# FFN gate and up by Strassen's scheme from column block 2 on, with its sums on VectorE and the down projection one gate block later

## The reference, cut to what matters

```python
def swiglu(h, w_gate, w_up, w_down):
    return (jax.nn.silu(h @ w_gate) * (h @ w_up)) @ w_down

x = x + swiglu(rms_norm(x, norm_ffn[l]), w_gate[l], w_up[l], w_down[l])
```

## Time and profile before

| what | value |
|---|---|
| time of 3 runs, median (lowest to highest) | 1870.86 us (1867.57 to 1871.2) |
| span of the profiled execution, slowest core | 1862.8 us |
| spans of the 8 cores | 1858.9 to 1862.8 us |
| TensorE matmul busy | 1723.7 us (93%), 10862 instructions |
| VectorE busy | 753.8 us (40%), 1521 instructions |
| ScalarE busy | 533.5 us (29%) |
| mean granted TensorE clock | 0.975 to 0.977 |

### The profile page before, as it was taken

How to read it: one execution, slowest core, us unless ns; L and a number is a source line. 1 busy time by engine, 2 the same in 40 slices (tenths; PEclk the granted TensorE clock), 3 DMA queues, 4 the chain that set the end, 5 groups by cost and what they waited for, 6 DMA issues and landing times.

```text
span 1862.8 us, 30031 instructions; the slowest of 8 cores (1858.9 to 1862.8 us)
## 1 busy us (share of the span) xinstructions
PE 1723.7 (93%) x10862; PEld 936.7 (50%) x10862; DVE 753.8 (40%) x1521; ACT 533.5 (29%) x921; POOL 102.2 (5%) x150
## 2 busy tenths in 40 slices
PE   4899999999986678997799999999999999999998
PEld 2565546666653237874344444444444444444444
DVE  3542124566566443434544151514325151423415
ACT  2442344877777352224450000000000000000000
POOL 0100000000001320000000000000000000000000
PEclk9899999999998889998899999999999999999999
DMA  9911634322316449147225507355270816446154
GB/s 219 250 47 24 115 69 78 77 53 41 81 42 135 127 113 210 46 81 122 46 46 91 91 12 125 49 88 86 50 123 14 136 28 109 63 74 104 32 91 181
DMA packets 40399, 166.17 MB, mean 89 GB/s; under 512 B 6208, under 2 KB 22208, under 8 KB 22336
## 3 DMA queue, kind: packets, MB, share of 16 engines
q0 software_dynamic: 17616, 111.32, 35.3%
q1 hardware_dynamic: 22640, 52.93, 9.2%
HBM read 258.18 MB, written 8.52 MB: 143 GB/s over the span
## 4 chain that ended last, share of the span: by engine, by line
PE 82%; DMA 5%; DVE 5%; ACT 4%; issue 3%; SPq 0%; POOL 0%; DVEq 0%; ACTq 0%; POOLq 0%
PE bank L1408 16%; PE pair L1405 16%; PE pair L1488 8%; PE bank L1488 8%; PE bank L521 5%; PE pair L521 4%; PE bank L1246 4%; DMA arena<-sel 3%; PE pair L850 3%; PE bank L829 2%; PE bank L698 2%; PE bank L703 2%; PE pair L1299 1%; PE pair L1246 1%; DMA arena<-wblk 1%
## 5 line engine op out<-in xcount | busy, mean ns | idle before, releaser
L1408 PE MATMUL bank<-arena 128*128 128x512 bf16 x1408 | 318.7, 379 | 0.0
L1405 PE MATMUL pair<-arena 128*128 128x512 bf16 x1344 | 303.8, 379 | 0.0
L1411 ACT ACTIVATE arena<-pair 128x512 bf16<-128x512 f32 x84 | 50.1, 597 | 806.4 <-PE pair L1405 786.6
L1412 DVE TENSOR_TENSOR arena<-bank,arena 128x512 bf16<-128x512 f32 x88 | 60.9, 692 | 537.9 <-PE pair L1405 411.0
L839 ACT ACTIVATE arena<-bank,arena 128x512 bf16<-128x512 f32 (+3 forms) x402 | 214.5, 573 | 72.0 <-PE pair L850 29.9
L1408 PEld LDWEIGHTS bank<-arena 128*128 128x128 bf16 x1408 | 137.6, 98 | 165.5
L1405 PEld LDWEIGHTS pair<-arena 128*128 128x128 bf16 x1344 | 131.5, 98 | 158.5
L1488 PE MATMUL pair<-arena 128*128 128x512 bf16 x704 | 166.3, 379 | 0.0
L1488 PE MATMUL bank<-arena 128*128 128x512 bf16 x704 | 166.3, 379 | 0.0
L850 PE MATMUL pair<-arena 128*128 128x129 bf16 (+1 forms) x1184 | 122.5, 223 | 17.2 <-DVE arena L843 15.0
L1491 DVE TENSOR_TENSOR arena<-pair,arena 128x512 f32<-128x512 f32 x176 | 121.8, 692 | 29.7 <-DVE arena L1491 23.8
(11 more groups left out here) (175 smaller groups left out, 1616.6 us busy)
## 6 DMA issues: line engine op xcount, KB each, us to landing
arena<-wblk POOLq DMA_DIRECT2D x106, 1024.0 KB, 12.5
arena<-xc SPq DMA_DIRECT2D x24, 1024.0 KB, 13.0
arena<-arena SPq DMA_DIRECT2D x64, 135.0 KB, 2.5
y<-arena SPq DMA_DIRECT2D x8, 1024.0 KB, 3.8
arena<-sel SPq DMA_DIRECT2D x28, 256.0 KB, 3.8
arena<-memb SPq DMA_DIRECT2D x2, 1024.0 KB, 5.5
arena<-cbf SPq DMA_DIRECT2D x1, 360.2 KB, 26.5
arena<-pvec SPq DMA_DIRECT2D x1, 219.0 KB, 9.9
```

Of the source, the lines that this page charges most:

```text
L1405: op(PE, lambda: nc.tensor.matmul(bank[pg][:, :], lhsT=wgt[:, kc, cc * 128:(cc + 1) * 128], rhs=hb[:, kc, :], start=(kc == 0), stop=(kc == ...
L1408: op(PE, lambda: nc.tensor.matmul(bank[pu][:, :], lhsT=wut[:, kc, cc * 128:(cc + 1) * 128], rhs=hb[:, kc, :], start=(kc == 0), stop=(kc == ...
L1412: op(DVE, lambda: nc.vector.tensor_tensor(out=actT[aj][cc][:, tc * 512:(tc + 1) * 512], in0=bank[pu][:, :], in1=sgt[sj][:, :], op=ALU.mult ...
```

## The change

From `jb` 2 on, each weight block (gate or up, 2048 x 256) times all 1024 activations is done as a 2 x 2 by 2 x 2 block product in Strassen's manner (Winograd's form): 7 products of half size, each 8 matmuls of 128x512 with a depth of 1024, so 56 matmuls where there were 64. The sums of activations are made once (`act_sums`, 3 VectorE instructions on 128x4096, and `act_diffs`, 2 of them in place). The sums of weights are made for every block by VectorE, 5 instructions of 128x1024 bf16 (`weight_sums`: three into `w3`, two in place in the slot), each emitted between the steps of the block before (`nxt`). The products go through four banks, here S, P, Q and R (banks 4 to 7); S, P and Q take two products each. Their combination takes one ScalarE copy and 6 VectorE instructions in fp32, then 4 times Silu (ScalarE, gate) or a multiply (VectorE, up). Gate and up of a `jb` now stand apart, one whole block of 56 matmuls after the other. The down projection of `jb` 2 and 3 runs after the gate block of `jb` 4, and so on; it is itself unchanged. The core of the diff:

```diff
+        def act_sums():
+            for k, (a, b) in enumerate((((0, 0), (1, 1)), ((0, 0), (0, 1)), ((1, 0), (1, 1)))):
+                op(DVE, lambda: tt_(out=b3[k], in0=B[a[0]][a[1]], in1=B[b[0]][b[1]], op=ALU.add), r=[h3[0][1], h3[1][1]], w=[b3b[k]] if k != 1 else [], pw=[b3b[k]] if k == 1 else [])
+        def weight_sums(n, wt, wb):
+            A = [[wt[:, 8 * k:8 * k + 8, 128 * f:128 * f + 128] for k in range(2)] for f in range(2)]
+            W, Wb = w3[n % 2], w3b[n % 2]
+            def s(k, a, b):
+                return lambda: op(DVE, lambda: tt_(out=W[:, k, :, :], in0=a, in1=b, op=ALU.add), r=[wb], w=[Wb[k]])
+            def d(a, b):
+                return lambda: op(DVE, lambda: tt_(out=a, in0=a, in1=b, op=ALU.subtract), r=[wb], pw=[wb])
+            return [s(2, A[0][0], A[0][1]), s(1, A[1][0], A[1][1]), s(0, A[0][0], A[1][1]), d(A[1][0], A[0][0]), d(A[0][1], A[1][1])]
+            product(S_, A[1][1], wb, B[1][0], Bb[1][0], True)
+            op(ACT, lambda: nc.scalar.copy(out=s4[:, :], in_=bank[S_][:, :]), r=[bankb[S_]], w=[s4b])
+            product(P_, W[:, 2, :, :], Wb[2], B[1][1], Bb[1][1], True)
+            op(DVE, lambda: tt_(out=dd[:, :], in0=s4[:, :], in1=bank[P_][:, :], op=ALU.subtract), r=[s4b, bankb[P_]], w=[ddb])
+            nxt()
+            product(S_, W[:, 1, :, :], Wb[1], B[0][0], Bb[0][0], False)
+            emit(bank[S_][:, :], bankb[S_], 1, 0)
+            nxt()
+            product(Q_, W[:, 0, :, :], Wb[0], b3[0], b3b[0], True)
+            op(DVE, lambda: tt_(out=ee[:, :], in0=bank[Q_][:, :], in1=dd[:, :], op=ALU.add), r=[bankb[Q_], ddb], w=[eeb])
+            op(DVE, lambda: tt_(out=ee[:, :], in0=ee[:, :], in1=bank[S_][:, :], op=ALU.subtract), r=[bankb[S_]], w=[eeb])
+            nxt()
+            product(P_, A[0][0], wb, B[0][1], Bb[0][1], False)
+            emit(bank[P_][:, :], bankb[P_], 0, 1)
+            op(DVE, lambda: tt_(out=ee[:, :], in0=ee[:, :], in1=bank[P_][:, :], op=ALU.add), r=[bankb[P_]], w=[eeb])
+            nxt()
+            product(R_, A[1][0], wb, b3[1], b3b[1], True)
+            op(DVE, lambda: tt_(out=ee[:, :], in0=bank[R_][:, :], in1=ee[:, :], op=ALU.add), r=[bankb[R_]], w=[eeb])
+            emit(ee[:, :], eeb, 1, 1)
+            nxt()
+            product(Q_, A[0][1], wb, b3[2], b3b[2], False)
+            op(DVE, lambda: tt_(out=cc_[:, :], in0=bank[Q_][:, :], in1=dd[:, :], op=ALU.add), r=[bankb[Q_], ddb], w=[ccb])
+            emit(cc_[:, :], ccb, 0, 0)
+        for jb in range(2, 22):
+            for gate in (True, False):
+                wt, wb, i = cur
...
+                    if gate:
+                        nx = wtaken()
+                    else:
+                        d_ = wtaken()
+                        nx = wtaken()
+                    todo = weight_sums(n + 1, nx[0], nx[1])
+                seven(n, wt, wb, aj, gate, todo)
+                wdone(i)
...
+                    if len(pairs) == 2:
+                        down(pairs)
+                        pairs = []
+                cur = nx
+        down(pairs, last=True)
```

More of the change, by code:

```diff
@@ L209, in buf @@
         return b
-    ARENA_BYTES = 204 * 1024
+    ARENA_BYTES = 207 * 1024
     def arena_init(self):
@@ L1454, in build @@
         rot_proj = Rot([0, 1, 2, 3])
[L1455 to L1480, removed]
+        FS = self.scope()
@@ new lines, in build @@
+        b3 = [HB[1][:, 8 * k:8 * k + 8, :] for k in range(2)] + [self.tile(FS, "b3", [128, 8, 512], BF16)]
+        b3b = [HBb[1], HBb[1], self.buf("b3")]
+        w3 = [self.tile(FS, f"w3_{j}", [128, 3, 8, 128], BF16) for j in range(2)]
+        w3b = [[self.buf(f"w3_{j}_{k}") for k in range(3)] for j in range(2)]
+        sg4 = sqt + [self.tile(FS, f"sg4_{j}", [128, 512], BF16) for j in range(2)]
+        sg4b = sqtb + [self.buf(f"sg4_{j}") for j in range(2)]
+        s4, dd, ee, cc_ = [self.tile(FS, n, [128, 512], F32) for n in ("s4", "dd", "ee", "cc")]
@@ new lines, in build @@
+        s4b, ddb, eeb, ccb = [self.buf(n) for n in ("s4", "dd", "ee", "cc")]
+        B = [[h3[t][0][:, 8 * k:8 * k + 8, :] for t in range(2)] for k in range(2)]
+        Bb = [[self.buf(f"B{k}{t}") for t in range(2)] for k in range(2)]
+        tt_ = nc.vector.tensor_tensor
+        def act_sums():
+            for k, (a, b) in enumerate((((0, 0), (1, 1)), ((0, 0), (0, 1)), ((1, 0), (1, 1)))):
+                op(DVE, lambda: tt_(out=b3[k], in0=B[a[0]][a[1]], in1=B[b[0]][b[1]], op=ALU.add), r=[h3[0][1], h3[1][1]], w=[b3b[k]] if k != 1 else [], pw=[b3b[k]] if k == 1 else [])
@@ new lines, in act_diffs @@
+        def act_diffs():
+            for (k, t), (k2, t2) in (((1, 0), (0, 0)), ((0, 1), (1, 1))):
+                op(DVE, lambda: tt_(out=B[k][t], in0=B[k][t], in1=B[k2][t2], op=ALU.subtract), r=[h3[t2][1]], w=[Bb[k][t], h3[t][1]])
+            for k in range(2):
+                _add(Bb[k][k].w, list(h3[k][1].w.values())[0])
+        def weight_sums(n, wt, wb):
[6 more added lines that the diff above has]
+            return [s(2, A[0][0], A[0][1]), s(1, A[1][0], A[1][1]), s(0, A[0][0], A[1][1]), d(A[1][0], A[0][0]), d(A[0][1], A[1][1])]
@@ new lines, in product, with seven, emit, nxt @@
+        def product(bi, lhs, lhsb, rhs, rhsb, fresh):
+            for k in range(8):
+                op(PE, lambda: nc.tensor.matmul(bank[bi][:, :], lhsT=lhs[:, k, :], rhs=rhs[:, k, :], start=(fresh and k == 0), stop=(k == 7), skip_group_check=True), r=[lhsb, rhsb], w=[bankb[bi]])
+        def seven(n, wt, wb, aj, gate, behind):
+            A = [[wt[:, 8 * k:8 * k + 8, 128 * f:128 * f + 128] for k in range(2)] for f in range(2)]
+            W, Wb = w3[n % 2], w3b[n % 2]
+            S_, P_, Q_, R_ = 4, 5, 6, 7
+            def emit(src, srcb, f, t):
+                j = 2 * f + t
+                if gate:
+                    op(ACT, lambda: nc.scalar.activation(out=sg4[j][:, :], in_=src, func=AF.Silu), r=[srcb], w=[sg4b[j]])
+                else:
+                    op(DVE, lambda: tt_(out=actT[aj][f][:, t * 512:(t + 1) * 512], in0=src, in1=sg4[j][:, :], op=ALU.mult), r=[srcb, sg4b[j]], w=[actTb[aj][f][t]])
+            def nxt():
+                if behind:
+                    behind.pop(0)()
+            product(S_, A[1][1], wb, B[1][0], Bb[1][0], True)
[21 more added lines that the diff above has]
+            emit(cc_[:, :], ccb, 0, 0)
+            while behind:
+                nxt()
@@ L1481, in build, with down @@
+        def down(pairs, last=False):
             for tt in range(8):
@@ L1485, in build @@
                     n_ = 0
-                    for (a_, wd_, wdb_, _) in dheld:
+                    for (a_, wd_, wdb_, _) in pairs:
                         for cc in range(2):
@@ L1491, in build @@
                     op(DVE, lambda: nc.vector.tensor_tensor(out=dst, in0=bank[psi][:, :], in1=dst, op=ALU.add), r=[bankb[psi]], w=[xrb[h][tt % 4][2 * cb4], xrb[h][tt % 4][2 * cb4 + 1]])
-                if jb == 21:
+                if last:
                     ob_ = self.buf(f"out{tt}")
@@ L1495, in build, with wtaken @@
                     self.outtoks.append((ob_.dsem, ob_.dcnt))
-            for d_ in dheld:
+            for d_ in pairs:
                 wdone(d_[3])
-            dheld = []
+        def wtaken():
+            wt, wb = wget()
+            return wt, wb, self.wcur - 1
+        act_sums()
+        for jb in range(2):
+            ia, (wgt, wgb_), ib, (wut, wub) = wgu[jb]
+            for cc in range(2):
+                drain(glu(jb, wgt, wgb_, wut, wub, cc, 1, rot_g.next(), rot_u.next()))
+            wdone(ia)
+            wdone(ib)
+        act_diffs()
+        pairs = []
+        for a_ in range(2):
+            wdt, wdb, i = wtaken()
+            pairs.append((a_, wdt, wdb, i))
+        cur = wtaken()
+        for f_ in weight_sums(0, cur[0], cur[1]):
+            f_()
+        down(pairs)
+        pairs = []
+        n = 0
+        for jb in range(2, 22):
+            aj = jb % 2
+            for gate in (True, False):
+                wt, wb, i = cur
+                todo = []
+                if gate or jb < 21:
+                    if gate:
+                        nx = wtaken()
+                    else:
+                        d_ = wtaken()
[3 more added lines that the diff above has]
+                wdone(i)
+                n += 1
+                if not gate:
+                    if jb == 21:
+                        d_ = wtaken()
+                    pairs.append((aj, d_[0], d_[1], d_[2]))
+                else:
+                    if len(pairs) == 2:
+                        down(pairs)
+                        pairs = []
+                cur = nx
+        down(pairs, last=True)
         self.mark("out")
```

## The result

The changed kernel takes 1946.1 us where the kernel before takes 1871.0 in the same comparison: ratio 1.0399, 95% interval 1.0378 to 1.042, slower by 75 us. The forecast was 1962 us, a loss of 91; the measured time lies in the range of 1920 to 2020.

What follows compares the result with a forecast made beforehand. The prediction took TensorE's matmuls to bound the kernel. Its terms, -69.1 + 111.6 + 14.8 + 26.3 + 5.9 + 1.5 = +91.0 us, on 1870.9 gave 1962 us, range 1920 to 2020.

Steps and rivals of the forecast that it cites:

- 320 matmuls: Gate and up blocks: 8 matmuls fewer in each of 40 blocks, at 0.2159 us each, -69.1 us.
- nine holds: Up block after a down projection: VectorE's weight sum waits for gt5 and TensorE stops, 9 x 12.4 = +111.6 us.
- clock in the gate block: Gate block after each TensorE stop for gt5: half clock costs 2.9 us, 9 x 2.9 = +26.3 us.
- steady waits: Next block's first product waits for the last in-place weight sum: 1.2 us per up, 0.25 per gate block, +14.8 us.
- start: First down projection: its adds wait on VectorE behind act_diffs and five weight sums, +5.9 us.
- end: Last down projection: its third matmul waits for the last combination and multiply, +1.5 us.
- The rival in which the clock stays up: TensorE keeps full clock after the nine stops for gt5: 1936 us, chance 0.15.
- VectorE's steady work: Up block's sums, combinations and multiplies laid out step by step on VectorE: next block starts 1.2 us late.
- the rival of 1.22 us: Each weight sum on VectorE takes 1.22 us, not 0.69: 59 us more, 2021 us, chance 0.15.
- the faster rival: In the up block after a down projection, gt5 lands before its wait stops TensorE: 1835 us, chance 0.03.
- The 8.1 us between span and time: Whole kernel: median of the runs lies 8.1 us above the 1862.8 us span, so the forecast starts from 1870.9.

Runs made afterwards that it cites:

- the first fill: The changed kernel with 36 unused matmuls ahead of the seventh product of nine up blocks, those where TensorE waits for gt5's sums: 1943.6 and 1940.2 us.
- the down projection at once: The changed kernel with the down projection again right after the up block of the odd column block: 1851.6 us, ratio 0.9907 to the kernel before.
- the run with the gate block first: The changed kernel with only the weight transfers reordered, the next gate block ahead of the down block: 1834.1 us, ratio 0.9821 to the kernel before.

## Why the prediction was right, and where a size was off

It forecast a slower kernel by one mechanism, and the runs show that mechanism: gt5 lands 17.5 us after the down projection in the period above (16.6 forecast), VectorE stands 13.06 us before its sum, TensorE stops after six products for 9.66 us. Over the nine periods of core 5 VectorE stands 11.8 us on average (12 forecast) and TensorE 8.4 (8.9 forecast). Taking only the transfers' order away gives back 112 us; the place of the down projection alone costs the kernel before 54.

The terms of the sum, with what core 5 measured:

| term | forecast | measured |
|---|---|---|
| 320 matmuls | -69.1 | 320 fewer, at 1.73 us for 8 as before: -69.1 |
| nine holds | 9 x 12.4 = 111.6 | 75.7 waiting for bank Q, 15.2 before the gate block, 14.4 for the seventh product at half clock, 2.9 of modelled ends: 108.2 |
| clock in the gate block | 9 x 2.9 = 26.3 | 1.56 to 1.97 in six of nine, nothing in three: 10.4 |
| steady waits | 14.8 | 10 x 1.02 + 11 x 0.21, 3.4 of modelled ends: 15.9 |
| start | 5.9 | 6.0, and 1.9 of half clock after it: 8.1 |
| end | 1.5 | 1.5 |

"Modelled ends" are 0.16 us for each pause: a pause is listed from the modelled end of a matmul, 0.16 us after the next one could have started. The measured column sums to 75.0 us, and the stage took 75.4 more. So the forecast of 91 was 16 us too high, and the clock is all of it: the holds came out 3 us shorter, the start and the steady waits 3 us longer.

- **The step that was mis-sized** is the clock: "I take that 2.9 us once a hold", 26.3 us in all, where 10.4 were measured. The clock did fall to 0.50 (1.2 GHz) in the hold, as in the earlier trace rows, but in the period above the gate block's first 24 matmuls took 6.90 us where 5.34 is full pace, 1.6 us more; and in three of the nine periods they took no more than full pace behind a like hold:

```profile
1158.45 5.34 PE L1491 MATMUL pair<-arena 128*128 128x512 bf16 x24 [1.61 <-DVE arena L1486]
```

  The windows view of core 5 over the end of the hold and the gate block's first 4.7 us (busy times, clock, DMA share, GB/s) shows the clock coming back within them:

```profile
1248.20:1251.00 2.80, 1.75 (x5) 0.68 (x6) 2.20 (x4) 0.00 (x0) 0.51 (x1) 0.50 1.08 164
1251.00:1254.00 3.00, 3.00 (x12) 1.20 (x11) 0.00 (x0) 0.59 (x1) 0.00 (x0) 0.76 1.03 167
```

  In the earlier trace rows 2.9 us were lost, which at 0.2159 us a matmul means half clock for some 13 of the 16; here it was 7 of 24. The rival in which the clock stays up was wrong too. Over all eight cores the gate block lost time behind 58 of 72 holds. The forecast also left out that the seventh product itself would run at half clock: it took 3.57 us out of the pause before the gate block, which was 1.6 to 2.0 us and not the 3.5 forecast, and so cost nothing.
- **The hold's length depends on the core.** The forecast took its landing from one period of one core. On cores 0, 2, 4 and 6 TensorE waited 53 to 55 us for bank Q in all, on 1, 3, 5 and 7 75 to 77. The slowest core sets the time. The one period read was of a core (7) that gets gt5 late, 15.8 us after its issue in that period; core 6 got it after 13.4 to 14.3. That the late kind was read is luck: the prediction did not look at the other cores.
- **VectorE's steady work**, laid out step by step from spacings of 0.60 and 0.79 us, was right within 0.2 us a block: the next block started 1.18 us late by count (1.02 of idle and 0.16 of modelled end), 1.2 forecast. The weight sums took 0.68 us, 0.69 forecast, by carrying the 256 to 512 element rows on to 1024; the rival of 1.22 us is out.
- **In place of the faster rival** stands its own condition, fulfilled by other means: once gt5 is issued early the kernel takes 1834 us, and the prediction had 1835 for a covered hold.
- **The 8.1 us between span and time** are not what lies around an execution. In the runs on record the time is 1.0 to 1.4 us above the span of the slowest core; so the profiled execution of the kernel before, with a span of 1862.8, was a short one of about 1864 us. The forecast isn't harmed by this, since it added its 91 us to the median of the runs.

## What to carry to other kernels

When work on the operands of the next step is put into an in-order engine's list in the middle of this step, the time by which that operand must have landed moves forward by a whole step, and everything behind the wait stops with it. So before such a change, list for each transfer when it can be issued (whose slot it takes, and what stands ahead of it in its queue) and when its first reader now comes; here two entries in the wrong order were worth 112 us, more than the 69 that the algorithm saves. And a dependency kept for a whole buffer is worth splitting where the reader and the writers touch different parts: 25 us here.

## What the runs showed of the hardware that was not expected

- In each pair of neighbouring cores (0 and 1, 2 and 3, and so on) one gets its weight blocks later than the other. The second block of five landed about 13 us after its issue on cores 0, 2, 4 and 6 in most periods and 15 to 17 on 1, 3, 5 and 7; the spans are 1915.7 to 1919.2 and 1939.4 to 1943.7 us. Which of the two is late differs from run to run: with the first fill, cores 1, 2, 4 and 7 were the late ones. In the kernel before, where TensorE waits for none of these blocks, the difference is there too on some pairs (second block after 13.4 to 14.3 us on core 6, 15.8 to 16.6 on core 7), and the profiled cores lie within 4 us of each other.
- Behind a pause in dense work the next matmuls sometimes run at half clock and sometimes don't, at the same length of pause. With the down projection at once, TensorE pauses nine times for 1.99 us on each core; 28 of these 72 pauses are followed by 1.5 to 1.7 us of lost time, the other 44 by none. Two of core 0 (the matmuls right behind the pause, then the next eight):

```profile
1251.80 1.46 PE L1543 MATMUL bank<-arena 128*128 128x512 bf16 x6 [1.99 <-DVE arena L1503]
1253.09 1.89 PE L1543 MATMUL pair<-arena 128*128 128x512 bf16 x8
...
1332.20 1.46 PE L1543 MATMUL bank<-arena 128*128 128x512 bf16 x6 [1.99 <-DVE arena L1503]
1333.49 3.58 PE L1543 MATMUL pair<-arena 128*128 128x512 bf16 x8
```

  With the first fill 24 of 28 pauses of 3.3 us had half clock behind them and 4 did not. Behind the 160 pauses of 1.0 to 1.4 us in the run with the gate block first no time was lost. What decides between the two outcomes was not tried.
